# The ScalarE half of a weight split, issued as two activations of 1024 columns with a signal each

## What is computed

```
# block 1
proj = rms_norm(x) @ w_in;  mix = concat(nsa(proj), retention(proj))
h = x + mix @ w_out
h = h + square(relu(rms_norm(h) @ w_up)) @ w_down
# block 2 (modulated by vectors computed from c @ w_ada)
proj = ln(h)*(1+sc1)+sh1 @ w_in_2;  y_a = mlstm(proj) @ w_down_m;  val, gate = gelu(s5(proj)) @ w_s5_glu
y = sigmoid(ga)*y_a + sigmoid(gb)*(val*sigmoid(gate));  x = ln(ALPHA*h + (1+g1)*(y @ w_mix_out))
val, gate = ln(x)*(1+sc2)+sh2 @ w_ffn_up;  x = ln(ALPHA*x + (1+g2)*((gelu(conv(gate))*val) @ w_ffn_down))
```

## Time and profile before

| what | value |
|---|---|
| time, median of 3 runs | 1797.97 us (1798.02, 1792.55, 1797.97) |
| the profiled execution's own time | 1795.44 us |
| its span | 1793.7 us |
| PE busy | 1560.9 us, 87% |
| DVE busy | 1114.7 us, 62% |
| POOL busy | 641.9 us, 36% |
| ACT busy | 576.5 us, 32% |
| mean granted clock of PE | 0.936 |

### The profile page before, as it was taken

How to read it: one execution, slowest core, us unless ns; L and a number is a source line. 1 busy time by engine, 2 the same in 40 slices (tenths; PEclk the granted TensorE clock), 3 DMA queues, 4 the chain that set the end, 5 groups by cost and what they waited for, 6 DMA issues and landing times. The chain is left out here.

```text
span 1793.7 us, 19497 instructions
## 1 busy us (share of the span) xinstructions
PE 1560.9 (87%) x6984; PEld 1220.4 (68%) x6984; DVE 1114.7 (62%) x1839; ACT 576.5 (32%) x779; POOL 641.9 (36%) x456
## 2 busy tenths in 40 slices
PE   3999899789999989979998884567994899999995
PEld 3778556678888778867666652346883788888874
DVE  5644377538699887376999999754636432232236
ACT  3333266034322222242332220553331433333231
POOL 2343100044555546424433330102543344444442
PEclk9999789899999999989999996788997899999998
DMA  6222100234555443212222212022321122223221
GB/s 261 76 90 71 46 2 1 94 135 141 188 188 188 156 173 137 96 61 94 100 106 71 101 51 88 24 71 106 141 106 59 59 94 99 89 99 113 91 74 47
DMA packets 37302, 178.75 MB, mean 100 GB/s; under 512 B 4192, under 2 KB 5088, under 8 KB 22496
## 3 DMA queue, kind: packets, MB, share of 16 engines
q1 hardware_dynamic: 31968, 168.15, 26.8%
q10 hardware_dynamic: 5248, 9.44, 1.5%
HBM read 166.04 MB, written 10.49 MB: 98 GB/s over the span
## 5 line engine op out<-in xcount | busy, mean ns | idle before, releaser
L1135 POOL TENSOR_TENSOR wlo<-raw,whi 128x512 fp32r<-128x512 f32 x448 | 628.7, 1435 | 1109.8 <-ACT whi L756 1109.8
L412 PE MATMUL bank<-Ahi,whi 128*128 128x512 f32 x1152 | 472.9, 410 | 3.2 <-POOL wlo L1135 2.3
L413 PE MATMUL bank<-Alo,whi 128*128 128x512 f32 x1152 | 452.2, 393 | 0.0
L414 PE MATMUL bank<-Ahi,wlo 128*128 128x512 f32 x1152 | 451.9, 392 | 0.0
L412 PEld LDWEIGHTS bank<-Ahi,whi 128*128 128x128 f32 x1152 | 219.2, 190 | 60.7 <-issue 11.2
L413 PEld LDWEIGHTS bank<-Alo,whi 128*128 128x128 f32 x1152 | 218.6, 190 | 54.7 <-issue 10.8
L414 PEld LDWEIGHTS bank<-Ahi,wlo 128*128 128x128 f32 x1152 | 218.4, 190 | 46.7
L756 ACT ACTIVATE whi<-raw 128x2048 fp32r<-128x2048 f32 x112 | 214.3, 1913 | 70.5 <-DMA raw<-in_ws 62.6
L412 PE MATMUL bank<-Bhi,whi 128*128 128x512 f32 x560 | 222.0, 396 | 9.4 <-DVE Blo L1635 5.8
L414 PE MATMUL bank<-Bhi,wlo 128*128 128x512 f32 x560 | 219.0, 391 | 0.0
L413 PE MATMUL bank<-Blo,whi 128*128 128x512 f32 x560 | 219.0, 391 | 0.0
(11 more groups left out here) (364 smaller groups left out, 2008.0 us busy)
## 6 DMA issues: line engine op xcount, KB each, us to landing
raw<-in_ws SPq DMA_DIRECT2D x112, 1024.0 KB, 4.9
adaw<-in_ada SPq DMA_DIRECT2D x48, 512.0 KB, 4.2
spill<-stage ACTq DMA_DIRECT2D x32, 256.0 KB, 2.0
X<-in_x SPq DMA_DIRECT2D x8, 512.0 KB, 4.9
gates<-spill SPq DMA_DIRECT2D x16, 256.0 KB, 5.2
w1k<-in_w1k SPq DMA_DIRECT2D x1, 2048.0 KB, 15.4
w1v<-in_w1v SPq DMA_DIRECT2D x1, 2048.0 KB, 19.6
XM<-spill SPq DMA_DIRECT2D x8, 256.0 KB, 2.9
```

The costliest lines, as they stand in the source:

```text
L412: pe.matmul(ps[:], wh, hi[:, k], start=(k == 0), stop=False)
L413: pe.matmul(ps[:], wh, lo[:, k], start=False, stop=False)
L414: ins = pe.matmul(ps[:], wl, hi[:, k], start=False, stop=(k == kn - 1))
L1135: pool.tensor_tensor(wlo[slot][:, part], raw[slot][:, part], rd(whi[slot][:, part]), ALU.subtract).then_inc(sem("lo_split"), 1)
```

## The change

ACT rounds each tile in two activations of 1024 columns instead of one of 2048, and signals `hi_split` after each, so the semaphore counts halves. POOL waits for the first half before its first two subtractions, and for the second half before its last two. In POOL's loop the waits are against a register value; there are now two for each tile. Nothing else is moved: ACT's waits before the rounding, the signals to PE and to SP, and the buffers are as they were.

```
-                    act.activation(whi[n % 2][:], raw[n % RAW][:], ACT.Copy).then_inc(sem("hi_split"), 1)
+                    for half in range(2):
+                        part = slice(1024 * half, 1024 * half + 1024)
+                        act.activation(whi[n % 2][:, part], raw[n % RAW][:, part], ACT.Copy).then_inc(sem("hi_split"), 1)
...
-                        pool.wait_ge(sem("hi_split"), pair * 2 + (a + slot + 1))
                         for q in range(4):
                             part = slice(512 * q, 512 * q + 512)
+                            if q % 2 == 0:
+                                pool.wait_ge(sem("hi_split"), pair * 4 + (2 * (a + slot) + q // 2 + 1))
                             pool.tensor_tensor(wlo[slot][:, part], raw[slot][:, part], rd(whi[slot][:, part]),
                                                ALU.subtract).then_inc(sem("lo_split"), 1)
```

## The result

| what | before | after |
|---|---|---|
| median of 6 runs each, side by side on one chip | 1794.5 us (1789.92 to 1798.02) | 1805.08 us (1803.48 to 1808.69) |
| the profiled execution's own time | 1795.44 us | 1805.89 us |
| its span | 1793.7 us | 1804.1 us |
| mean granted clock of PE | 0.936 | 0.929 |

The ratio is 1.006, 95% interval 1.0046 to 1.0074: slower by 10.6 us, where +9.6 us and 1806 us were predicted. Lines of the changed kernel stand two or three further down: L756 is now L758, L1135 is L1138, L1095 is L1097, L1929 to L1933 are L1932 to L1936, L1212 is L1215, L1828 is L1831.

A forecast was written before the change was run, and what follows sets the result against it. PE waits far longer for DVE than for low parts; the gated chain has no slack. 6.8 + 2.9 + 1.5 + 0.8 + 0.3 - 2.7 = +9.6 us, giving 1805.0 or 1807.6 by base; predicted 1806, range 1797 to 1813.

The forecast's parts named there:

- POOL starts 0.85 us sooner: POOL's subtractions in each tile: start 1.14 us after the rounding's start, 0.85 us sooner than before.
- A hit costs 0.98 us: DVE instructions with two SBUF operands: the next one begun after POOL's start takes 1.67 us instead of 0.69.
- The gated products, +6.8: Gated products: L1929 is newly hit, lengthening a chain without slack by 0.98 us in seven rounds, +6.8 us.
- The second feed-forward part, +2.9: Second feed-forward part: the last Blo is hit, lengthening PE's pauses at three group ends by 0.98 us each, +2.9 us.
- The clock behind the last pause, +1.5: Last group end, second feed-forward part: pause grows to 3.08 us, clock likelier than not falls, losing 7 matmuls, +1.5 us.
- The first mLSTM head, +0.8: First mLSTM head: the cast grows from 0.43 to about 1.4 us, XCl shrinks to about 1.66, PE waits, +0.8 us.
- Given back, -2.7: Start, norms, first products and the 2.30 us pause: POOL's earlier end saves collisions or waiting, -2.7 us, bounds 0 and -5.
- The state-space part, 0 within 3: State-space part, where PE waits for DVE: collisions appear and vanish alike, 0 us, bounds about -3 and +3.
- R1: Gated products: chain has slack or L1929 is not hit, no 6.8 us; 1798 to 1801, no change; chance 0.16.
- R2: State-space part: more collisions vanish than appear, each worth 0.98 us; with 10 of 13 about 1797; chance 0.08.
- R3: Gated products and state-space part: two or three more 1.2 GHz stretches, 1.5 us each, +13 to +14, 1811; chance 0.12.
- R4: POOL's start does not move, its register-value wait resolving late; only ACT's 0.3 us remain, 1798; chance 0.06.

The follow-up runs named there:

- e3: Changed kernel with the early POOL start only in tiles 68 to 75 (gated products), whole-tile wait elsewhere; 1801.39 us, 1.0037 against the kernel before.
- e4: Changed kernel, all tiles early, plus a second buffer for the evicted gv product; 1800.24 us, 1.0031 against the kernel before.
- e5: Changed kernel with the first activation of 512 columns, the second 1536; 1819.0 us, 1.0136 against the kernel before.
- e6: Changed kernel with the first activation of 1536 columns in all tiles; 1797.13 us, 1.0011 against the kernel before.
- e2: Changed kernel, but POOL waits for the whole tile in tiles 68 to 75 (gated products); 1801.26 us, 1.0024 against the kernel before.
- e7: Changed kernel with the early POOL start only in tiles 80 to 111 (second feed-forward part); 1795.24 us, 1.0003 against the kernel before.
- e13: Changed kernel with first activation of 1792 columns, early start only in tiles 0 to 65, and spare gv buffer; 1791.96 us, 0.9985 against the kernel before.
- e8: Changed kernel with the early POOL start only in tiles 0 to 65, through most of the state-space part; 1796.9 us, 1.0014 against the kernel before.
- e12: Kernel before with only a second buffer for the evicted gv product added; 1794.92 us, 1.0004 against the kernel before.
- e1: Changed kernel, two activations kept, but POOL waits for the whole tile everywhere; 1794.42 us, 0.9996 against the kernel before.
- e11: Changed kernel with the early POOL start only in tiles 66 and 67, one at the first mLSTM head; 1795.58 us, 1.0003 against the kernel before.
- e10: Changed kernel with first activation of 1536 columns, early start only in tiles 0 to 65, and spare gv buffer; 1785.12 us, 0.9949 against the kernel before.

## Why the prediction was right, point by point

**POOL starts 0.85 us sooner: right.** 1.13 us behind the rounding's start, where 1.14 was worked out. The two activations take 2.00 us together, not 2.12.

**A hit costs 0.98 us, for the next SBUF instruction of DVE: right in size here, and not a fixed price.** It is 1.67 against 0.69 in the change, in e3, e4 and e5, and the seven gated rounds lost 6.7 us, 0.96 each. The first subtraction of POOL's four, alone, in the round shown of the changed kernel and of e6:

```profile
1244.42 1.58 POOL L1138 TENSOR_TENSOR wlo<-raw,whi 128x512 fp32r<-128x512 f32 x1 [5.20 <-ACT whi L758]
...
1233.33 1.29 POOL L1137 TENSOR_TENSOR wlo<-raw,whi 128x512 fp32r<-128x512 f32 x1 [5.20 <-ACT whi L757]
```

The last 0.69 us of L1932, which is what it takes undisturbed, begin at 1244.88 + 1.67 - 0.69 = 1245.86, and the subtraction ends at 1246.00. In e6 it is 1233.36 + 1.81 - 0.69 = 1234.48 and 1234.62. So the hit instruction stands still until 0.14 us before the running subtraction ends. The same holds for every one of the 818 TENSOR_TENSOR instructions with two 128x512 SBUF operands that took over 0.3 us more than in the profile where they were shortest, over all fourteen profiles: the gap is 0.13 to 0.15 us each time, while the delays go from 0.3 to 1.15 us. A hit costs what is left of the subtraction when the DVE instruction comes. The Trainium skill ("SBUF — State Buffer", Who interferes with whom) has the shared port pair as an exclusive lock, where whoever issues first keeps it for the whole instruction and the other fully blocks, the latter said of DVE's two-port modes. The trace agrees with such a lock for these instructions too, with the 0.14 us beside it. The prediction set that rule against the row, as the 1.43 us mean of a subtraction for each hit, 10.0 us for seven; but a blocked instruction waits for the rest of the other, not for its full length.

**The gated products, +6.8: right**, +6.7 in the profile and 0.37% when made alone (e3). This was the term that decided the sign and the size.

**The second feed-forward part, +2.9: right in the pauses, wrong in the sum.** They are 1.74, 1.73 and 3.09 us, each 1.0 longer, as the rows said. But the part grew by 1.7 only. The step that failed is that the three pauses are the whole effect; the missing 1.3 is at the part's head. The two stretches from 1410 us on, behind the norm:

```profile
1410.00:1413.40 3.40, 3.39 (x11) 2.89 (x12) 3.19 (x7) 2.21 (x3) 0.00 (x0) 0.56 0.65 270
1413.40:1416.80 3.40, 3.40 (x17) 2.78 (x16) 2.74 (x6) 0.91 (x2) 0.00 (x0) 1.00 0.00 0
```

and the same two in the kernel before:

```profile
1401.30:1404.70 3.40, 3.40 (x10) 2.87 (x11) 3.19 (x7) 2.26 (x3) 0.00 (x0) 0.50 0.69 280
1404.70:1408.10 3.40, 3.40 (x11) 2.71 (x10) 2.69 (x6) 0.86 (x2) 0.00 (x0) 0.64 0.00 0
```

At 0.64 the second has 11 matmuls, at 1.00 it has 17: six at 0.21 us each, 1.3 us, come back because the lower clock ends sooner. The same is seen in e2, e4, e5 and e7. It is seen in e13 too, and in part in e8, where POOL has its old start here, so it isn't shown that the earlier start is what ends the lower clock. The prediction looked for the clock behind the last pause and not here.

**The clock behind the last pause, +1.5: wrong.** It grew to 3.09 us as foreseen, and the granted clock stayed at 1.00. The step that failed is the inference from one pause of 2.30 us with a fall behind it that a longer one would have one too. The kernel before already spoke against it: behind its pause of 2.51 us, which ends at 995.43, the clock stayed up (the first row below). The same group end of e13, with a pause of 2.10 us as before the change, is followed by the lower level from 1.3 us behind the pause on (the second row), and that of e5, with 4.08 us, at once (a clock of 0.50 with 8 matmuls in 3.40 us). The length of the last pause doesn't decide it, so the rows gave no ground to call the fall likelier than not.

```profile
995.50:998.90 3.40, 3.40 (x12) 2.13 (x13) 3.25 (x4) 0.00 (x0) 3.37 (x3) 1.00 0.00 0
...
1738.30:1741.70 3.40, 3.40 (x10) 2.63 (x9) 1.41 (x1) 0.36 (x1) 3.40 (x4) 0.51 0.00 0
```

**The first mLSTM head, +0.8: right there, open in what follows.** The timeline, against the earlier trace rows:

```profile
1124.75 4.58 POOL L1138 TENSOR_TENSOR wlo<-raw,whi 128x512 fp32r<-128x512 f32 x3 [44.53 <-ACT whi L758]
...
1125.15 1.37 DVE L1829 CAST XCh<-CA 128x512 fp32r<-128x512 f32 x1
1126.56 1.63 DVE L1831 TENSOR_TENSOR XCl<-CA,XCh 128x512 fp32r<-128x512 f32 x1
...
1128.24 0.80 PE L412 MATMUL bank<-XCh,whi 128*128 128x512 f32 x1 [6.82 <-DVE XCl L1831]
```

The cast is hit (1.37, was 0.43) and the first matmul comes 0.8 us later in its stage. Another 1.7 us appear in the rest of the mLSTM part. The seven us behind that matmul have a mean granted clock of 0.63, where the same seven before have 0.75, which would be a share of it. But e12, whose only edit is the buffer of the gated products, takes 102.60 us for this part, 1.6 more than the kernel before, with a clock of 0.66 in the same seven us. So the 1.7 can't be put down to the change. The head itself moves the other way with a later start: where POOL waits for the whole tile, 0.09 us later than before, the stretch up to that matmul is 11.60 us instead of 12.70.

**Given back, -2.7: wrong.** The small instruction of the first norm did fall from 1.19 to 0.17 us, and the first product came 1.4 us sooner, where 0.9 was taken; it comes at 32.6 to 33.5 us in the five kernels with an earlier start of 512 or 1024 columns and at 33.8 or later in all others, so this much is real. But the first products then took 2.1 us longer, with ten hits where there were six. The step that failed is that the prediction counted two waits that would shorten and no hits that would come. The hits are not the earlier start's alone: e1, e7 and e11, whose POOL starts 0.09 us later than before, have nine, ten and nine, and e3 has eight. The pause for a low part went from 2.30 to 1.31 and now ends with an eviction, without the slow stretch of the earlier trace rows, which is more than the 0.4 taken; the pause behind it grew from 4.51 to 6.75 and took all of it. By the end of the state-space part the two executions are level (1114.76 and 1114.75 us), so nothing was given back up to there. The norm ahead of the second feed-forward part did give 0.5, where 0.4 was taken. The text said that the next pause "takes most of it"; it took more.

**The state-space part, 0 within 3: right**, -1.0, one hit fewer of 29. It is within what executions of one start differ by. The bound was too narrow for the size of first part next to it: e6 gained 5.6.

**The sum.** +9.6 was predicted and +10.5 found in the profile. Charged too much: the clock's 1.5 and 1.2 in the second feed-forward part, 2.7 together. Missing: 1.7 in the mLSTM part, and of the -2.4 for what is given back and the longer rounding only -0.5 is there (the state-space part's -1.0 in it), 3.6 together. So that the forecast came so close is in part luck, errors of both signs, and the smaller of these lie within what one execution differs from another by. Its largest term is not luck. Of the rivals, R1 is out (L1932 is hit), R2 is out for this change though e6 and e10 show the mechanism at work, R3 is out (no fall behind the pauses of the gated products or the three longer group ends), and R4 is out (the start moved).

## What to carry to other kernels

Idle time of an engine that is not the bound is no reason to start it sooner: ask which instructions of the other engines it will then run beside, and price each by the slack of the chain behind it. A hit lasts as long as what is left of the other engine's running instruction. One collision cost 0.96 us where the chain was tight, and nothing where one spare buffer gave it slack. When the start of a background engine can be moved, try several positions and choose stage by stage, since the effect goes in steps and changes sign. And profile a kernel whose edit doesn't touch a stage before a difference of 1 or 2 us in that stage is explained.

## What the runs showed of the hardware

- In e6 POOL began at 1233.33, 0.03 us ahead of a product, and that product took 1.81 us, 0.14 more than the usual hit of 1.67, since nearly the whole subtraction was still to come. A hit doesn't need a DVE instruction that was already running.
- A hit DVE instruction stands still until 0.13 to 0.15 us before the running subtraction ends, in all 818 cases of fourteen profiles.
- TENSOR_TENSOR instructions of DVE with an operand in PSUM were never hit: 350 of them (128x512) began 0.3 us or more before the end of a running subtraction, in the fourteen profiles, and none took over 0.1 us more than its shortest.
- Several hits in a row don't grow: the three of e5 are 1.69, 1.67 and 1.66 us, against 0.69 undisturbed.
- POOL pays as well. Four subtractions took 5.03 us in e1 with DVE idle beside them, and 6.39 in the round shown of the changed kernel.
- The granted clock stayed at 1.00 behind a pause of 3.09 us and fell to 0.52 behind one of 2.30; behind a pause of 2.10 us at the same place it stayed up in the kernel before and fell to 0.51 in e13. The length of the last pause alone doesn't tell.
- Two activations of 1024 columns, one behind the other, take 2.00 us, and one of 2048 took 1.91. The split costs 0.09 us.
